# Two token groups side by side in two PSUM banks: the matmuls of the up, branch, output and down projections alternate between them

## The reference, cut to what matters

```python
xn = rmsnorm(x, attn_pre_norm)
h = xn @ w_in                        # 1024 -> 5716 columns, split into q, k, v, gates ...
gla_o = gated_linear_attention(...)  # 4 heads
dsa_o = sparse_attention(...)        # 8 query heads, top-k keys
mixed = (gate_a * (gla_o @ w_branch_gla) + gate_b * (dsa_o @ w_branch_dsa)) @ w_out
x = x + rmsnorm(mixed, attn_post_norm)
hc = causal_conv3(rmsnorm(x, ffn_pre_norm) @ w_up)      # 1024 -> 5632
a, b = split(hc)
f = (gelu(a) * b) @ w_down                              # 2816 -> 1024
x = x + rmsnorm(f, ffn_post_norm)
```

## Time and profile before

| what | value |
|---|---|
| median of 3 runs | 1033.92 us (1033.77 to 1034.04) |
| span of the profiled execution | 1030.1 us, first to last instruction; its own time is not listed apart from the three runs |
| median less span | 3.8 us, outside the first and last instruction |
| TensorE busy | 1008.6 us, 98% |
| VectorE busy | 549.9 us, 53% |
| ScalarE busy | 389.9 us, 38% |
| DMA | 104.25 MB, 101 GB/s on average |

### The profile page before, as it was taken

The page is one execution under the profiler, slowest core; times in us unless marked ns, Lnnn a source line. Parts: engine busy times, 40 slices in busy tenths (PEclk is TensorE's granted clock), DMA queues, the critical chain, the costliest instruction groups (busy, mean ns, idle before and its releaser), DMA issues.

```text
span 1030.1 us, 17281 instructions
## 1 busy us (share of the span) xinstructions
PE 1008.6 (98%) x6878; PEld 951.7 (92%) x6878; DVE 549.9 (53%) x852; ACT 389.9 (38%) x672; POOL 80.5 (8%) x237
## 2 busy tenths in 40 slices
PE   5999999999999999999999999999999999999997
PEld 5989999888999999999998899999999999888886
DVE  5248978745232336743445668666666666312214
ACT  6334336666322136532124545333333333312212
POOL 4100000000010001102001001000000001100000
PEclk9999999999999999999999999999999999999999
DMA  7612211111222224347446452232222232312233
GB/s 242 152 42 83 70 55 42 47 59 41 96 76 65 64 66 162 126 143 238 149 127 218 138 157 82 81 81 81 81 81 81 81 82 83 125 62 82 86 109 112
DMA packets 103956, 104.25 MB, mean 101 GB/s; under 512 B 13634, under 2 KB 88242, under 8 KB 103904
## 3 DMA queue, kind: packets, MB, share of 16 engines
q1 hardware_dynamic: 97600, 81.06, 26.4%
q0 software_dynamic: 6304, 22.47, 6.2%
HBM read 89.84 MB, written 13.67 MB: 100 GB/s over the span
## 4 chain that ended last, share of the span: by engine, by line
PE 94%; ACT 2%; DVE 1%; issue 1%; DMA 1%; SPq 0%; ACTq 0%; DVEq 0%
PE ps L1380 19%; PE ps L1382 19%; PE ps L1381 19%; PE ps L1389 7%; PE ps L1391 7%; PE ps L1390 7%; PE ps L1543 2%; PE ps L1521 2%; PE ps L1468 2%; PE ps L1460 2%; PE ps L1399 1%; PE ps L1400 1%; PE ps L1529 1%; PE ps L1505 1%; PE ps L1578 1%
## 5 line engine op out<-in xcount | busy, mean ns | idle before, releaser
L1380 PE MATMUL ps<-xs,whi 128*128 128x288 f32 x1312 | 392.5, 299 | 0.2 <-issue 0.2
L1382 PE MATMUL ps<-xs,wlo 128*128 128x288 f32 x1312 | 386.6, 295 | 0.0
L1381 PE MATMUL ps<-xs,whi 128*128 128x288 f32 x1312 | 386.3, 294 | 0.0
L1380 PEld LDWEIGHTS ps<-xs,whi 128*128 128x128 f32 x1312 | 246.2, 188 | 1.8 <-issue 0.8
L1381 PEld LDWEIGHTS ps<-xs,whi 128*128 128x128 f32 x1312 | 246.2, 188 | 0.8 <-issue 0.2
L1382 PEld LDWEIGHTS ps<-xs,wlo 128*128 128x128 f32 x1312 | 246.1, 188 | 0.0
L1035 DVE TENSOR_TENSOR wlo<-raw,whi 128x2048 fp32r<-128x2048 f32 (+2 forms) x45 | 99.5, 2212 | 133.2 <-ACT whi L706 133.0
L706 ACT ACTIVATE whi<-raw 128x2048 fp32r<-128x2048 f32 (+2 forms) x47 | 86.2, 1834 | 100.4 <-PE ps L1391 88.1
L1389 PE MATMUL ps<-whi,xs 128*128 128x256 f32 (+2 forms) x264 | 85.9, 325 | 0.0
L1390 PE MATMUL ps<-whi,xs 128*128 128x256 f32 (+2 forms) x264 | 83.0, 315 | 0.0
L1391 PE MATMUL ps<-wlo,xs 128*128 128x256 f32 (+2 forms) x264 | 83.0, 314 | 0.0
(11 more groups left out here) (264 smaller groups left out, 1534.0 us busy)
## 6 DMA issues: line engine op xcount, KB each, us to landing
raw<-in_w_up SPq DMA_DIRECT2D x44, 512.0 KB, 4.7
raw<-in_w_in SPq DMA_DIRECT2D x21, 1024.0 KB, 5.6
raw<-in_w_down SPq DMA_DIRECT2D x10, 1024.0 KB, 5.1
raw<-in_w_out SPq DMA_DIRECT2D x6, 1024.0 KB, 5.2
gate_scratch<-stage POOLq DMA_DIRECT2D x16, 288.0 KB, 2.6
gates_in<-gate_scratch POOLq DMA_DIRECT2D x8, 576.0 KB, 4.2
raw<-in_w_branch_gla SPq DMA_DIRECT2D x4, 1024.0 KB, 5.2
silu_scratch<-stage POOLq DMA_DIRECT2D x8, 288.0 KB, 4.6
```

Source lines behind the costliest of these rows:

```text
L1380: pe.matmul(out, wh[:, k, c0:c0 + P], xh[:, k, t], start=(k == 0), stop=False)
L1381: pe.matmul(out, wh[:, k, c0:c0 + P], xl[:, k, t], start=False, stop=False)
L1382: ins = pe.matmul(out, wl[:, k, c0:c0 + P], xh[:, k, t], start=False, stop=(k == kn - 1))
```

## The change

The two halves of a branch or up unit, and two prompt tiles of an output or down job, are now written side by side: each matmul of the one is followed by the same matmul of the other, in the other bank. Both matmuls of such a couple use the same weight block. Sample tile 0 stays alone. The counts, shapes and operands of all matmuls stay; only their order, the place of the bank waits (both banks before the pair) and the signals (two `wide_done` on the last two matmuls of the pair) change. The input projections keep the old form. The first-pass `up` calls also keep it.

```diff
+            def stationary_pair(outs, p, kn, n, c0, xh, xl, halves):
+                wh, wl = half_of(whi, p, kn, n), half_of(wlo, p, kn, n)
+                for k in range(kn):
+                    for out, t in zip(outs, halves):
+                        pe.matmul(out, wh[:, k, c0:c0 + P], xh[:, k, t], start=(k == 0), stop=False)
+                    for out, t in zip(outs, halves):
+                        pe.matmul(out, wh[:, k, c0:c0 + P], xl[:, k, t], start=False, stop=False)
+                    for out, t in zip(outs, halves):
+                        ins = pe.matmul(out, wl[:, k, c0:c0 + P], xh[:, k, t], start=False, stop=(k == kn - 1))
+                return ins
+
+            def moving_pair(outs, p, k0, kn, n, xh, xl, his, los, first, last):
...
+                for k in range(kn):
+                    for out, t in zip(outs, his):
+                        pe.matmul(out, xh[:, k0 + k, t], wh[:, k, :], start=(first and k == 0), stop=False)
+                    for out, t in zip(outs, los):
+                        pe.matmul(out, xl[:, k0 + k, t], wh[:, k, :], start=False, stop=False)
+                    done = [pe.matmul(out, xh[:, k0 + k, t], wl[:, k, :], start=False, stop=(last and k == kn - 1))
+                            for out, t in zip(outs, his)]
+                return done
...
             def wide(job, both, xh, xl, prompt_hi, prompt_lo):
-                for t, tt in enumerate(job.tiles):
+                sample = [t for t, tt in enumerate(job.tiles) if tt == 0]
+                prompts = [t for t, tt in enumerate(job.tiles) if tt != 0]
+                for group in [sample] * bool(sample) + [prompts[i:i + 2] for i in range(0, len(prompts), 2)]:
+                    outs = [ps[:, job.banks[t], :] for t in group]
                     if job.first:
-                        wait_bank(job, t)
-                        if job.panel == DOWN0 and job.banks[t] < 4:
-                            pe.wait_ge(h_ready, 2 * KF)
+                        for t in group:
+                            wait_bank(job, t)
+                            if job.panel == DOWN0 and job.banks[t] < 4:
+                                pe.wait_ge(h_ready, 2 * KF)
...
                     if job.last:
-                        ins.then_inc(wide_done, 1)
+                        for d in done:
+                            d.then_inc(wide_done, 1)
...
-                        up(r, g, 0)
-                        up(r, g, 1).then_inc(unit_done, 1)
+                        stationary_pair([ps[:, 4 * (1 - r) + 2 * g + t, 0:HALF] for t in range(2)], UP0 + r, KD, 256, P * g, xhi, xlo,
+                                        [slice(HALF * t, HALF * t + HALF) for t in range(2)]).then_inc(unit_done, 1)
```

More of the change, by code:

```diff
@@ L1383, in stationary_weights @@
                 return ins
+            def stationary_pair(outs, p, kn, n, c0, xh, xl, halves):
[9 more added lines that the diff above has]
+            def moving_pair(outs, p, k0, kn, n, xh, xl, his, los, first, last):
+                wh, wl = half_of(whi, p, kn, n), half_of(wlo, p, kn, n)
+                done = []
+                for k in range(kn):
[6 more added lines that the diff above has]
+                return done
             def moving_weights(out, p, k0, kn, n, xh, xl, t, first, last, tl=None):
@@ L1612, in _ @@
                         pe.wait_ge(unit_free[u % 2], u // 2 + 2 * q)
[L1613 to L1616, removed]
+                        stationary_pair([ps[:, 2 * (u % 2) + j, 0:HALF] for j in range(2)], BRANCH0 + g, kn, 256, P * m, xh, xl,
+                                        [slice(HALF * j, HALF * j + HALF) for j in range(2)]).then_inc(unit_done, 1)
@@ L1618, in wide @@
             def wide(job, both, xh, xl, prompt_hi, prompt_lo):
                 open_panel(job.panel)
-                for t, tt in enumerate(job.tiles):
+                sample = [t for t, tt in enumerate(job.tiles) if tt == 0]
+                prompts = [t for t, tt in enumerate(job.tiles) if tt != 0]
+                for group in [sample] * bool(sample) + [prompts[i:i + 2] for i in range(0, len(prompts), 2)]:
+                    outs = [ps[:, job.banks[t], :] for t in group]
                     if job.first:
-                        wait_bank(job, t)
-                        if job.panel == DOWN0 and job.banks[t] < 4:
-                            pe.wait_ge(h_ready, 2 * KF)
-                    if tt == 0:
-                        ins = moving_sample(ps[:, job.banks[t], :], job.panel, job.k0, job.kn, 512, both, job.first, job.last)
-                    else:
-                        ins = moving_weights(ps[:, job.banks[t], :], job.panel, job.k0, job.kn, 512, xh, xl, prompt(tt, prompt_hi),
-                                             job.first, job.last, prompt(tt, prompt_lo))
+                        for t in group:
+                            wait_bank(job, t)
+                            if job.panel == DOWN0 and job.banks[t] < 4:
+                                pe.wait_ge(h_ready, 2 * KF)
+                    if group == sample:
+                        done = [moving_sample(outs[0], job.panel, job.k0, job.kn, 512, both, job.first, job.last)]
+                    else:
+                        done = moving_pair(outs, job.panel, job.k0, job.kn, 512, xh, xl, [prompt(job.tiles[t], prompt_hi) for t in group],
+                                           [prompt(job.tiles[t], prompt_lo) for t in group], job.first, job.last)
+                    ins = done[-1]
```

## The result

The changed kernel takes 1037.87 us by the median of 4 runs (1036.95 to 1038.22), the kernel before, run again beside it, 1033.85: a ratio of 1.0043 with a 95% interval of 1.003 to 1.0055. It is slower, by 4.0 us where 2.8 were forecast.

A forecast was written before the change was run, and what follows sets the result against it. TensorE, busy 98% of the span, was taken to bound the kernel through the distance between matmul starts. Terms 0 + 1.9 + 0.9 + 0 = +2.8 us on 1033.9 gave 1036.7 us, range 1033.5 to 1039.9.

The forecast's parts named there:

- Part 1: Paired matmuls in all projections: bank changes cost and save nothing, the pace stays; 0, bounds -3.4 and +2.9 us.
- Part 2: Kernel end: tiles 3 and 4 finish one matmul apart, so VectorE takes tile 4 later; +1.9 us.
- Part 3: Output to up projection: TensorE waits longer for VectorE's copy of job 7's tile 3; +1.2, net +0.9 us.
- Part 4: Other set ends (jobs 1, 3, 5, down projection's first half): later hand-overs are covered; 0, perhaps to +0.5 us.
- the bank rival: Stationary pairs: sustained bank alternation removes the excess per matmul; 993 us if taken whole, chance 0.10.
- The mixed order has another pace: Paired matmuls: pace shifts up to 1 ns either way; 1039.6 (chance 0.15) or 1033.3 us (chance 0.13).
- the forecast case: Whole kernel: pace within 0.4 ns of before, tail and hand-over losses both present; 1035.4 to 1038.0 us, chance 0.50.
- The clock rival: Stationary pairs: short TensorE idles at bank changes lose the full clock; 1070 us if for a tenth, chance 0.02.

The follow-up runs named there:

- the up pairs alone: Kernel before with only the up projection's loop in pairs; 12 runs in two groups, medians 1028.4 and 1034.8 us.
- the operands alone: Changed kernel, but in the up loop both interleaved halves of a unit are summed into one bank; 1037.21 us, one run.
- the norm held back: Changed kernel, but VectorE writes tile 4's norm twice, meant to make TensorE wait at tile 4's transposes; 1038.43 us.
- the code shifted: Changed kernel with one more TensorE instruction, a wait on two long-reached semaphores, ahead of the up loop; 1037.77 us.
- the last pairs apart: Changed kernel, but tiles 3 and 4 of the last output and last down job one after the other; 1029.37 us, 0.9965 of the kernel before.
- the output pair apart: Changed kernel, but only job 7's tiles 3 and 4 of the output projection apart; seven of 12 runs 1029.99 to 1031.74 us, five 1037.01 to 1037.99.

## Why the prediction held, step by step

The time lies in the stated range, and parts 2 to 4 came by the mechanism that they name. Part 1, the pace, did not, and that the measured time still lies in the range is in part luck, as the last points say.

- *Part 2, the tail, +1.9:* 5.25 - 3.36 = 1.89 us, by the mechanism stated, two tiles 2.12 us apart on VectorE.
- *Part 3, the hand-over, +0.9:* 1.15 lost and 0.35 given back, +0.8. The first up matmul came 1.11 us later against job 7's last one (1.17 forecast), and the transposes lost their wait as forecast.
- *Part 4, the other ends, 0:* no new wait of TensorE; the output stage took the same time but for the hand-over, the down projection 0.08 us less.
- *Part 1, the pace, 0:* the step that was mis-sized, "I take the middle, 0". It cost 1.58 us in the up loop and 0.46 in the branch loop, 2.0 together, inside the bounds of -3.4 and +2.9; the 720 matmuls of 512 columns kept their pace (542 for 541 in the down window). The half that said that the bank explains nothing was right and is now shown for sustained alternation. The other half, "if each matmul carries its own cost the mean stays", is wrong: two kinds of place in turn give 133.3 or 130.0, neither of them the mean of 131.6 and 133.4. The bounds, taken from the spread of the two halves, held by luck on the quick side: 2.5 ns x 1920 is -4.8 us, more than -3.4.
- *The sum:* 2.0 + 1.9 + 0.8 - 0.1 = 4.6 us between the traces without the start's 0.5, and 4.0 between the medians. The 3.8 us added for what lies outside the span were 1.7 us outside and 2.1 us of a short execution. This did no harm, since the sum goes from the median before.
- *The range:* all four executions of the changed kernel had times of the slow group. With the quick pace it would take some 6.4 us less, 1031.5, below the range's 1033.5; that is an estimate from the two groups of the up pairs alone.
- *The rivals:* the bank rival is out. "The mixed order has another pace" is what came on top of the forecast case. The clock rival is out too: the granted clock stayed at 1.00 with an alternation in each matmul. The Trainium skill's page "TensorE: Matmul & The Clock Gate", section "A second HAM failure mode: psum-queue depth-cycling", tells of a kernel whose clock was lost while it cycled through banks; nothing of it shows here. The 2.5 ns over the columns that the same page of the Trainium skill gives in its section "Wait — 56ns, not 53.3ns?" did not appear in any order; the least seen at 288 columns is 10 ns (130.0).

What stays open: whether the changed kernel as it stands has the quick pace too. All 4 of its timed executions, and the one execution each of the operands alone, the norm held back and the code shifted, which keep both last pairs, were slow (7 of 7), while with job 7's tiles apart 16 of 29 executions of three kernels were quick. Equal odds in both would hardly give that, so something ahead of the loop may shift them; what draws the pace was not found. The traces have a hint. The unpaired matmuls just ahead of the up loop repeat intervals of about 132, 132, 133 and 136 ns. In the one quick trace the 136 is the last interval before the loop; in five of the six slow ones it is the fourth from the end, in the sixth (the up pairs alone) the second. The pace may be set by where in this period the loop is entered, but one quick trace does not show it. The 0.9965 of the last pairs apart rests on five quick executions and should not be counted on, since the output pair apart fell in the slow group 5 times in 12.

## What to carry to other kernels

Before giving each matmul another bank, look at a place where the program already changes banks: if the distance of starts is the same there, the bank is not what TensorE waits for. Finishing two results together moves the evacuation of the first out from under the matmuls of the second; at the end of a kernel and before a bank is reused that is paid, here 1.9 us and 1.1 us (0.8 once the transposes gave some back), and the last pair should stay apart. When TensorE is busy all the time, time the same shape at different places of its streamed operand, and take enough executions to see whether the times fall into groups.

## What was not expected of the hardware

- The place of the streamed operand: 288 fp32r columns that start at an even multiple of 128 bytes in the row and end at an odd one took 131.7 ns a matmul, those that start at an odd multiple and end at an even one 133.4, in either order; moved by 32 tokens, the slow half became quick. The widths of 320 and 256, which start and end at even multiples, had 13.5 and 13.2 ns above their columns, close to the 13.4 of the slow half.
- With the two kinds in turn the loop has two paces, 130.0 ns (129, 131) and 133.3 ns (131, 131, 132, 140), kept over the 1920 matmuls of the up loop in each trace, through loop branches and waits, and changing from execution to execution: 6.4 us in 1033, or 0.6%, between executions of one program with the same granted clock (0.997 to 0.999). The branch loop kept its slow pattern in the trace whose up loop was quick.
